# Two stacked transformer blocks on one core: all attentions but the cross one in groups of two pairs of tiles

## What is computed

```python
# first block, each layer, for each head and 128 queries
pc = softmax(where(mc, q @ kc.T * s, NEG))       # 31 compressed keys
ps = softmax(where(ms, q @ ks.T * s, NEG))       # selected keys (all causal ones here)
pw = softmax(where(mw, q @ kw.T * s, NEG))       # window of 512
out = g0 * pc @ vc + g1 * ps @ vs + g2 * pw @ vw
# convolution branch: layer norm over 512 channels, then silu and a projection
un = (u - mean) * rsqrt(var + EPS) * ln_g + ln_b
y_conv = silu(un) @ w_pw2
# second block: layer 0 has A (dense) and B (band of 128 with a sink), layer 1 has
# C (dense, 64 + 32 dimensions per head) and D (neighbourhood on a grid of 8 by 64),
# then in both a cross attention X (4 heads of 128, 256 keys) and a gated feed-forward
oa = softmax(qa @ ka.T * s) @ va
ob = softmax(concat(band(qb @ kb.T * s), sink))[:-1] @ vb
oc = softmax((qn @ kn.T + qr @ kr.T) * s) @ vc
od = softmax(where(valid, qd @ kd.T * s + bias, NEG)) @ vd
```

## Time and profile before

| what | value |
|---|---|
| median of 3 runs | 2256.18 us (2254.81 to 2256.32) |
| profiled execution | 2258.11 us, of which the profile's span is 2256.3 us |
| PE busy | 2183.1 us, 97% of the span |
| DVE, ACT, POOL busy | 1234.2, 1063.6, 852.7 us |
| mean granted TensorE clock | 0.987 of full speed |

### The profile page before, as it was taken

One profiled execution on the slowest core, in us unless ns is written; L12 is line 12 of the kernel. 1 busy time (PEld: TensorE's weight loads), 2 busy tenths in 40 slices (PEclk: granted clock), 3 DMA queues, 4 the chain that ended last, 5 costly groups with the idle time before them and its releaser, 6 DMA issues.

```text
span 2256.3 us, 32927 instructions
## 1 busy us (share of the span) xinstructions
PE 2183.1 (97%) x11938; PEld 1750.3 (78%) x11938; DVE 1234.2 (55%) x2642; ACT 1063.6 (47%) x2160; POOL 852.7 (38%) x665
## 2 busy tenths in 40 slices
PE   8999899999999999989999999999999999999997
PEld 6778667887876788667888888888767888888886
DVE  5997783389778546895562202234566655211222
ACT  6542475465247653585463323333366645332332
POOL 4433303444221243203345545554211425555553
PEclk9999999999999999999999999999999999999998
DMA  5334102333320233302333333333110413333332
GB/s 165 90 94 135 33 2 69 105 89 94 122 62 11 58 89 107 90 2 75 94 84 95 94 111 98 91 102 122 40 59 20 123 56 99 98 95 99 98 96 67
DMA packets 106895, 187.87 MB, mean 83 GB/s; under 512 B 12016, under 2 KB 22768, under 8 KB 106608
## 3 DMA queue, kind: packets, MB, share of 16 engines
q1 hardware_dynamic: 101136, 178.67, 27.4%
q10 hardware_dynamic: 5600, 7.11, 1.0%
HBM read 181.01 MB, written 2.10 MB: 81 GB/s over the span
## 4 chain that ended last, share of the span: by engine, by line
PE 85%; DVE 9%; issue 2%; ACT 2%; POOL 1%; DMA 0%; SPq 0%; DVEq 0%; ACTq 0%
PE bank L891 24%; PE bank L893 23%; PE bank L892 23%; PE bank L1120 3%; PE bank L1133 3%; PE bank L1106 2%; DVE temp L1978 1%; DVE bank L2097 1%; PE bank L898 1%; DVE temp L2010 1%; PE bank L1097 1%; PE bank L1100 1%; PE bank L961 1%; POOL w_lo L2256 1%; PE bank L1010 1%
## 5 line engine op out<-in xcount | busy, mean ns | idle before, releaser
L2256 POOL TENSOR_TENSOR w_lo<-w_raw,w_hi 128x512 fp32r<-128x512 f32 (+3 forms) x618 | 823.7, 1339 | 1319.9 <-ACT w_hi L1256 1319.5
L891 PE MATMUL bank<-op_hi,w_hi 128*128 128x512 f32 x1840 | 735.1, 400 | 9.6 <-POOL w_lo L2256 4.4
L893 PE MATMUL bank<-op_hi,w_lo 128*128 128x512 f32 x1840 | 720.8, 392 | 0.0
L892 PE MATMUL bank<-op_lo,w_hi 128*128 128x512 f32 x1840 | 720.8, 392 | 0.0
L1256 ACT ACTIVATE w_hi<-w_raw 128x512 fp32r<-128x512 f32 (+2 forms) x634 | 385.2, 617 | 683.2 <-PE bank L893 679.2
L891 PEld LDWEIGHTS bank<-op_hi,w_hi 128*128 128x128 f32 x1840 | 347.6, 189 | 95.9 <-issue 15.5
L893 PEld LDWEIGHTS bank<-op_hi,w_lo 128*128 128x128 f32 x1840 | 348.0, 189 | 74.1
L892 PEld LDWEIGHTS bank<-op_lo,w_hi 128*128 128x128 f32 x1840 | 348.0, 189 | 73.6 <-issue 4.1
L1673 DVE TENSOR_TENSOR temp<-bank,rstd 128x512 f32<-128x512 f32 x139 | 96.1, 692 | 366.7 <-PE bank L893 348.9
L891 PE MATMUL bank<-side_hi,w_hi 128*128 128x512 f32 (+1 forms) x628 | 233.2, 371 | 2.6 <-DVE side_lo L1772 1.4
L893 PE MATMUL bank<-side_hi,w_lo 128*128 128x512 f32 (+1 forms) x628 | 230.8, 368 | 0.0
(11 more groups left out here) (272 smaller groups left out, 2236.0 us busy)
## 6 DMA issues: line engine op xcount, KB each, us to landing
w_raw<-in_weights SPq DMA_DIRECT2D x620, 256.0 KB, 2.7
w_raw<-in_weights SPq DMA_DIRECT2D x32, 192.0 KB, 2.3
temp<-temp SPq DMA_DIRECT2D x40, 64.0 KB, 2.0
x_t<-in_x SPq DMA_DIRECT2D x8, 256.0 KB, 5.1
conv_area<-in_mem ACTq DMA_DIRECT2D x2, 1024.0 KB, 5.5
conv_area<-in_bias ACTq DMA_DIRECT2D x1, 2048.0 KB, 9.5
out_y<-ybuf SPq DMA_DIRECT2D x8, 256.0 KB, 2.1
w_raw<-in_weights SPq DMA_DIRECT2D x10, 128.0 KB, 2.2
```

The lines of the kernel that those rows point to most:

```text
L891: pe.matmul(dst, w[0], m[0], start=start, stop=False)
L892: pe.matmul(dst, w[0], m[1], start=False, stop=False)
L893: return pe.matmul(dst, w[1], m[0], start=False, stop=stop)
L2256: pool.tensor_tensor(w_lo[:, j, 0:n], w_raw[:, p % RAW_RING, 0:n], w_hi[:, j, 0:n].bitcast(F32), ALU.subtract).then_inc(*mark("weights_spl ...
```

## The change

In NSA, AB2, D2 and C2 the loop now runs over groups of two pairs; X2 stays as it was. In step s PE scores both pairs of group s, multiplies group s - 2 and turns group s - 1. DVE only inverts the sums; POOL scales the tiles (`probs_scaled`) with two scalars, the gate or a column of ones being the second; the compressed tiles stay on DVE. DVE copies tiles 1 and 3 of each group from PSUM, ACT tiles 0 and 2; the last four of NSA are all DVE's. The transposes go through three banks (4, 5 and the output's, in NSA bank 7 from tile 52 on) instead of two. E has 8 buffers instead of 6, PT's fourth buffer is `rstd`. Outputs of A, B and C are taken for two pairs at once. C's order interleaves chunks j and j + 1, so that the four 32-row matmuls of a group follow each other on four quarters of the partitions. The layer norm moves to bank 7 and its later steps come 4 to 9 tiles later; on POOL its squares and sums are spread over steps 4 to 7. The next part's low halves come one a step, from the sixth step before the end on. The warm matmuls of NSA go (3), AB2 has 2 at its first turn instead of 1. The cut diff:

```diff
-TURN_LAG = 2
-VALUE_LAG = 3
-OUT_LAG = 7
-LN_TILES = 44
-NORM_LAG = 3
-LOW_LAG = 2
-E_RING = 6
+PAIRS = {"NSA": 2, "AB2": 2, "D2": 2, "C2": 2, "X2": 1}
+TURN_LAG = {1: 2, 2: 1}
+VALUE_LAG = {1: 3, 2: 2}
+LN_TILES = 52
+LN_SQUARES = {4: (0,), 5: (1, 2), 6: (3,)}
+LN_ADDS = {6: ((0, 1),), 7: ((2, 3), (0, 2))}
+LOW_LAG = {1: 2, 2: 4}
+VECTOR_COPIES = (1, 3)
+E_RING = 8
-SCORES = (1, 2, 3)
-GATE_CHUNKS = (2, 1, 1, 4)
+SCORES = (1, 2, 3, 0)
+GATE_CHUNKS = (2, 2, 4)
-WARM_TURN = {"NSA": {30: 3}, "AB2": {0: 1}, "D2": {0: 2}, "C2": {0: 2}, "X2": {0: 2}}
+WARM_TURN = {"NSA": {}, "AB2": {0: 2}, "D2": {0: 2}, "C2": {0: 2}, "X2": {0: 2}}
...
-                for j in range(4):
-                    for i in range(NT):
+                order = [(j, i) for j in range(4) for i in range(NT)]
+                if kind == "C2":
+                    order = [(j + e, i) for j in (0, 2) for i in range(NT) for e in range(2)]
...
-        PT = [tmp(E_RING + i) for i in range(PT_RING)]
+        PT = [tmp(E_RING), tmp(E_RING + 1), tmp(E_RING + 2), rstd[:, :]]
...
+                    if PAIRS[step[1][0]] == 2:
+                        third = t["out"] if step[1][0] != "NSA" else 7 if n >= LN_TILES else 4
+                        t["turn"] = (4, 5, third, 4 if third != 4 else 5)[n % 4]
...
-                    at(37 + c, "ln_scale", l, c)
+                    at(44 + c + 2 * (c // 2), "ln_scale", l, c)
-                at(30, "ln_var", l)
-                at(32, "ln_factor", l)
-                at(35, "ln_spread_factor", l)
+                at(34, "ln_var", l)
+                at(36, "ln_factor", l)
+                at(40, "ln_spread_factor", l)
...
+        def by_vector(part, t):
+            n = t["a"] - ATT[part][0]["a"]
+            return grouped(part) and (n % 4 in VECTOR_COPIES or part[0] == "NSA" and n >= len(ATT[part]) - 4)
+        def scaled_by_pool(part, t):
+            return grouped(part) and not t["cmp"]
... PE
+                def latent_scores(group):
+                    parts = ((0, 0), (0, 1), (1, 0))
+                    ...
+                    for pair in group:
+                        free_banks(pair)
+                        for x, y in parts:
+                            for t in pair:
+                                pe.matmul(score_bank(t), t["q"][x], t["k"][y], start=(x + y == 0), stop=False)
+                    for x, y in parts:
+                        for t in group[0] + group[1]:
+                            ins = pe.matmul(score_bank(t), t["more"][0][x], t["more"][1][y], start=False, stop=(x == 1))
...
+                for s in range(steps_of(part)):
+                    if part[0] == "C2" and s < len(groups):
+                        latent_scores(groups[s])
+                    else:
+                        for pair in in_group(groups, s):
+                            scores(pair)
+                    ...
+                    if PAIRS[part[0]] == 2:
+                        for pair in in_group(groups, s - value_lag):
+                            values(pair)
+                    for pair in in_group(groups, s - turn_lag):
+                        for t in pair:
+                            turn(t)
... ACT, a group's step
+                        to_copy = [t for t in to_copy if not by_vector(part, t)]
+                        for t in to_exp[:1]:
+                            exps(t)
+                        for t in to_copy[:1]:
+                            copy(t)
+                        for t in to_exp[1:2]:
+                            exps(t)
+                        for t in to_copy[1:]:
+                            copy(t)
+                        for t in to_exp[2:]:
+                            exps(t)
... DVE
+                    if scaled_by_pool(part, t):
+                        dve.reciprocal(total, total).then_inc(*mark("sums_inverted", a))
+                        return
+                def copy(t):
+                    a = t["a"]
+                    dve.wait_ge(*after("probs_turned", a))
+                    ...
+                    dve.tensor_copy(PT[a % PT_RING][:, 0:n], bank[t["turn"]][:, 0:n]).then_inc(*mark("probs_copied_vector", a))
... DVE, a group's step
+                        for pair in before[:1]:
+                            normed(pair)
+                        for t in to_max[:2]:
+                            maxed(t)
+                        for pair in before[1:]:
+                            normed(pair)
+                        for t in to_max[2:3]:
+                            maxed(t)
+                        for t in [pair[1] for pair in in_group(groups, s - value_lag)]:
+                            if t["last"]:
+                                output(t)
+                        for t in to_copy[:1]:
+                            copy(t)
+                        for t in to_max[3:]:
+                            maxed(t)
+                        for t in to_copy[1:]:
+                            copy(t)
... POOL
+                def scaled(pair):
+                    t = pair[0]
+                    pool.wait_ge(*after("sums_inverted", pair[1]["a"]))
+                    total, _ = pair_sums(t)
+                    for r, t in enumerate(pair):
+                        e = E[t["a"] % E_RING][:, 0:t["nk"]]
+                        if t["gate"] is not None:
+                            ins = pool.tensor_scalar(e, e, total[:, r:r + 1], t["gate"], ALU.mult, ALU.mult)
+                        else:
+                            ins = pool.tensor_scalar(e, e, total[:, r:r + 1], C("ones")[:, 0:1], ALU.mult, ALU.mult)
+                        ins.then_inc(*mark("probs_scaled", t["a"]))
+                for s in range(steps_of(part)):
+                    for pair in in_group(groups, s - 1):
+                        if scaled_by_pool(part, pair[0]):
+                            scaled(pair)
+                    ahead = last_of(FOLLOWS[part] + 1)
+                    if len(groups) - 6 <= s < len(groups) - 2:
+                        split_to(min(state["split"], ahead))
+                    elif s == len(groups) - 2:
+                        split_to(ahead)
```

More of the change, by code:

```diff
@@ L632, in build @@
                     t["a"], t["g"] = at_tile, at_group
-                    banks = SCORES if step[1][0] == "NSA" and at_tile - ts[0]["a"] < LN_TILES else SCORES + (0,)
-                    t["bank"] = banks[(at_tile - ts[0]["a"]) % len(banks)]
+                    n = at_tile - ts[0]["a"]
+                    t["bank"] = SCORES[n % len(SCORES)]
                     t["held"] = held.get(t["bank"])
@@ L643, in build, with groups_of, lags_of, moments_of @@
                 ATT[step[1]] = ts
+        def groups_of(part):
+            n = 2 * PAIRS[part[0]]
+            return [[ATT[part][i + j:i + j + 2] for j in range(0, n, 2)] for i in range(0, len(ATT[part]), n)]
+        def lags_of(part):
+            return TURN_LAG[PAIRS[part[0]]], VALUE_LAG[PAIRS[part[0]]]
+        def moments_of(part, s):
+            n = 2 * PAIRS[part[0]]
+            return range(n * s, n * s + n)
+        def steps_of(part):
+            return len(groups_of(part)) + VALUE_LAG[PAIRS[part[0]]] + 2 - PAIRS[part[0]]
+        def in_group(groups, s):
+            return groups[s] if 0 <= s < len(groups) else []
         ENDS = 0
@@ L2013, in normed @@
                         ins.then_inc(*mark("probs", t["a"]))
+                def copy(t):
+                    a = t["a"]
+                    dve.wait_ge(*after("probs_turned", a))
+                    if part[0] == "NSA" and a == ts[PT_RING - 1]["a"]:
+                        evac(LAST_GATE[part[1]])
+                        dve.wait_ge(*taken(LAST_GATE[part[1]]))
+                    if a >= PT_RING:
+                        dve.wait_ge(*after("values", a - PT_RING))
+                    n = P * (1 if t["cmp"] else len(t["pv"]))
+                    dve.tensor_copy(PT[a % PT_RING][:, 0:n], bank[t["turn"]][:, 0:n]).then_inc(*mark("probs_copied_vector", a))
                 def output(t):
@@ new lines, in attend @@
+            def attend(part):
+                groups, l = groups_of(part), part[1]
+                def scaled(pair):
[6 more added lines that the diff above has]
+                            ins = pool.tensor_scalar(e, e, total[:, r:r + 1], t["gate"], ALU.mult, ALU.mult)
+                        else:
+                            ins = pool.tensor_scalar(e, e, total[:, r:r + 1], C("ones")[:, 0:1], ALU.mult, ALU.mult)
+                        ins.then_inc(*mark("probs_scaled", t["a"]))
+                if part[0] == "NSA":
+                    norm_added(l)
+                for s in range(steps_of(part)):
+                    for pair in in_group(groups, s - 1):
[6 more added lines that the diff above has]
+                        split_to(ahead)
+                    if part[0] == "NSA" and s in LN_SQUARES:
+                        for c in LN_SQUARES[s]:
+                            norm_square(l, c)
+                    if part[0] == "NSA" and s in LN_ADDS:
```

(2 more changed lines are left out.)

277 lines of the change are left out of this document (156 added, 121 removed).

## The result

The changed kernel took 2237.48 us (median of 6 runs, 2233.07 to 2239.98), the kernel before 2254.72 in its 6: a ratio of 0.9926, interval 0.9913 to 0.9939. That is 17 us, where the forecast took 45 off.

What follows compares the result with a forecast made beforehand. Prediction: PE bounds A, C2 and D2, DVE bounds B, no engine is full in NSA. NSA −26, A −4, B −4.5, D2 −3, C2 −9, fill +1.5 sum to −45: median 2211 us, range 2190 to 2244.

Steps and rivals of the forecast that it cites:

- Of the 13.3, DVE waits partly for PE ... I take 11: NSA: DVE's 13.3 us not busy between head and tail was to become 11 a layer.
- NSA's term: NSA: 112.7 us to become 99.7, −13 a layer, −26 for two; bounds −7 and −21 a layer.
- POOL's price: POOL scaling 128x512 with two scalars: 0.65 us taken, bounds 0.611 and 2.06; no row has it.
- the slower rival: POOL's scale at 2.06 bounds every 512-wide group; about 2288 us, chance 0.10; decides from near 1.75 per 512.
- the fill: Head of each of 5 parts: first transposes wait for POOL instead of DVE, 0.3 each, +1.5 us.
- C2: Attention stage C2: fewer changes of form and 32-row matmuls four at a time; −9 us, bounds −5.8 and −11.2.
- A: Attention stage A: grouped matmuls save PE 0.52 a group over 8 groups, group at 5.4; −4 us.
- B: Attention stage B: DVE stays fullest, 37.1 to 31.5 busy; −4.5 us taken, bounds 0 and −5.6.
- D2: Attention stage D2: 0.52 saved in each of 8 groups, the hop over POOL can show; −3 us, bounds 0 and −4.2.
- Smaller gain: POOL's scale at w_lo's price, 32-row matmuls two at a time, or in-order DVE waits in NSA; 2232 to 2234, chance 0.20.
- larger: PE alone paces NSA, −21 a layer, with C2 at −11: −64 us, 2190 to 2192; chance 0.10.
- no change: NSA paced by ACT and DVE handing over, gains come back as waits, POOL's price eats A and D2; chance 0.05.

Runs made afterwards that it cites:

- the run with the root apart: Changed kernel with the layer norm's mean square a group ahead of the steps behind ScalarE's root, spread and scaling a group later: 2234.18 us, ratio 0.9910.
- thin scale: POOL scales only 8 columns of each tile: in A, B, C2 and D2 of the changed kernel, 2238.51 us; in NSA of the spread kernel, 2211.58 us.
- the spread kernel: Changed kernel with NSA's low halves and layer norm centring, scaling and squares one a step, and the root's wait apart: 2220.61 us, ratio 0.9848.

## Why the prediction was wrong

**The step that failed is NSA's "Of the 13.3, DVE waits partly for PE ... I take 11".** Busy times came out as worked (76.3 for DVE, 93.5 for 91.5 on PE), but DVE's idle time in the middle was treated as a remainder that shrinks with the work. It grew: 25.3 and 26.4 in the two layers where 11 was taken. PE is busy for most of an ordinary step (4.54 of 4.80 at full clock in one of them, in the run with the root apart), and it waits in the steps in which DVE's extra work stands ahead of an inversion. That work was in the 76.3 by its sum alone; how much of it a step of four tiles takes at once was not counted. Laid out one piece a step it gives 17 us back, and NSA's term comes to −11.4 and −11.9 for −13. Even there DVE's idle time hardly shrinks (26.2 and 25.0, 26.9 and 26.2 before, in the first cut): of the 11.4 in layer 0, 10.7 is the work that DVE lost.

**The clock had no term in the sum.** The prediction read that a lower clock stretches PE's work in NSA's head and tail, and let the clock of the middle be. It fell from 0.98 to 0.90 in layer 0 and from 0.96 to 0.90 in layer 1. That makes PE's same work longer, as the step of 5.3 against 3.6 shows; the clock of the whole stage, 0.91 and 0.89, rose both where the stalls were filled (0.97 and 1.00) and where DVE's work was spread (0.97).

**POOL's price**, taken as 0.65, is 0.769 for 512 and 0.447 for 128. It is far from the 1.75 from which the slower rival decides, and hidden in C2 and nearly in A (with a thin scale its groups take 5.42, which took 5.42 to 5.59). In NSA it isn't hidden: the thin scale brings 4 to 5 us a layer in the spread kernel, which the sum had at nothing beyond the fill. The estimate from the GPSIMD Engine Reference of the Trainium skill ("Key points"), 1.1 for 512, was too dear for a scale with one tile read. VectorE's own scale of 512 columns took 0.635 in NSA before, with two scalars as well, and 0.484, with one scalar, at the head of B, where POOL did nothing: ratios of 1.2 and 1.6, not 2.

```profile
L2010 DVE TENSOR_SCALAR temp<-temp,small,gates 128x512 f32<-128x512 f32 x32 | 19.0, 635 | 0.6
```

The contention that SBUF — State Buffer of the Trainium skill ("Who interferes with whom") describes cost little where the prediction looked for it: the low halves of NSA took 0.68 to 0.77 in the mean of their groups, against 0.69 in NSA before. It shows elsewhere, between POOL's squares and the compressed pair's scaling (2.07 for 0.49, above).

**C2** was right in mechanism and size (−8.3 for −9), and the quarters bring 5.5 of it. **A** was right in its group (5.43 for 5.4). **B**'s group is 4.83 to 4.97, where 14 pairs took 36.7 before, 5.2 for two: 8 groups give 2.9 of the 4.5 forecast. POOL's hop is on its path: the thin scale gives 0.2 a group back, 1.7 of the 2.9 by which A with B fell short. **D2** gained 1.1 for 3. The hop over POOL, which the prediction named as its risk there, costs 0.14 a group; the bank that two tiles share, which stood at nothing, shows only when POOL is out of the way, as 0.18 in the transposes and 0.03 in the group. What keeps the group 0.2 above the 2.95 of PE's own blocks then is open.

**The rivals.** "Smaller gain" comes nearest (2232 to 2234). Its third condition, in-order DVE waits that keep NSA's pace, holds, but it meant copies that wait for their transpose. These waits are there (16.3 us in layer 0, and 18.8 in the spread kernel, which is 17 us faster); what the runs show to cost the time is the extra work ahead of the inversions. Its price, −7 a layer, was still too large a gain. Its other conditions, w_lo's price and 32-row matmuls two at a time, did not occur. "Slower" fell with POOL's price, "larger" with NSA's idle time, "no change" with the 17 us. Of the signs of being wrong, POOL's scale stayed under 1.35, PE waited for POOL ahead of some transposes (six waits, 4.5 us in layer 0), and DVE did wait in copies.

One step of the working is off without harm: at 1.375 POOL's four scales in A take 5.5, and A's group was 5.9 before, which leaves a gain of about 3 and not nothing. No term of the sum used it.

## What to carry to other kernels

When a loop takes bigger steps, work that was hung at single tiles falls in lumps: count what each in-order engine gets in each step, and what is queued behind it, before calling any of it free. Relieving the fullest engine by its busy time buys little where another waits for a few of its instructions; ask for both engines what they do in the longest steps, not in the mean one. Where a stall lowers TensorE's clock, its price is the wait and the slower work behind it: take the stall out before filling it.

## What the runs showed of the hardware

32-row matmuls on four quarters of the rows run four at a time (twelve in 0.90 in the changed kernel, against 1.59 on two quarters), and they do so too when the program issues six of one pair and then six of the other. POOL scaling a tile by two scalars costs 0.447 for 128 columns and 0.769 for 512, a quarter more than the one-input CAST of the earlier trace rows. In D2 eight transposes of four tiles took 1.10 with a bank for each, and 1.28 where two tiles share one (both with the thin scale). Two scalings of 128 columns on DVE took 2.07 beside two of POOL's squares (TENSOR_TENSOR), and 0.49 without them.
